# Attention in another order: all sequence items, then all memory items

## The reference

```python
u = rms_norm(x, g_mix) @ w_in            # split into lru, gate, q, k, v, qm
y_lru = rg_lru(conv(u_lru)) * gelu(u_gate)
q, k = rms_norm(u_q), rms_norm(u_k)      # 6 query heads, 2 key heads, 64 wide
y_swa = sliding_window_sink_attention(q, k, v, sinks)   # window 128, blocks of 128
mkv = rms_norm(mem, g_mem) @ w_mem_kv    # 256 memory tokens
y_mem = memory_cross_attention(qm, km, vm)              # 4 heads, softmax over 256
y = concat(rms_norm(y_lru), rms_norm(y_swa), rms_norm(y_mem))
h = x + y @ w_out
h = h + moe(rms_norm(h))                 # 32 experts, top 4 of a router
```

## Time and profile before

| | |
|---|---|
| time before, median of 3 runs | 2288.44 us (2286.68 to 2290.86) |
| time of the profiled execution | 2293.3 us |
| its span, first to last instruction | 2291.6 us |
| mean granted TensorE clock | 0.978 |
| busy: TensorE, its weight loads | 2175.5 us (95%), 1609.1 us (70%) |
| busy: VectorE, ScalarE, GpSimd | 1422.4 us (62%), 1094.1 us (48%), 227.6 us (10%) |
| attention and its token sums | 262.7 to 384.8 us |
| chain that ended last | TensorE 73%, VectorE 8%, issue 7%, ScalarE 6%, DMA 4% |

### The profile page before, as it was taken

The page is one execution under the profiler, slowest core; times in us unless marked ns, Lnnn a source line. Parts: engine busy times, 40 slices in busy tenths (PEclk is TensorE's granted clock), DMA queues, the critical chain, the costliest instruction groups (busy, mean ns, idle before and its releaser), DMA issues.

```text
span 2291.6 us, 31520 instructions
## 1 busy us (share of the span) xinstructions
PE 2175.5 (95%) x9748; PEld 1609.1 (70%) x9749; DVE 1422.4 (62%) x2152; ACT 1094.1 (48%) x1602; POOL 227.6 (10%) x208
## 2 busy tenths in 40 slices
PE   6999988996999999999999999999999999999997
PEld 4443776443578877776787878787778877887885
DVE  3342573334775677768767575768786657667665
ACT  3241452112464465556555454546565445445444
POOL 2000200002210011011101010110100110101001
PEclk9999997996999999999999999999999999999998
DMA  7000402002795589869958586858997658658556
GB/s 254 1 0 19 157 1 74 28 28 88 275 362 195 187 277 332 289 205 348 343 177 322 182 297 198 290 183 326 353 335 265 204 174 297 196 177 315 181 182 220
DMA packets 203190, 477.62 MB, mean 208 GB/s; under 512 B 14744, under 2 KB 20952, under 8 KB 203089
## 3 DMA queue, kind: packets, MB, share of 16 engines
q1 hardware_dynamic: 185662, 437.95, 52.7%
q0 software_dynamic: 17424, 39.17, 7.5%
q10 hardware_dynamic: 66, 0.02, 0.0%
HBM read 468.73 MB, written 32.11 MB: 219 GB/s over the span
## 4 chain that ended last, share of the span: by engine, by line
PE 73%; DVE 8%; issue 7%; ACT 6%; DMA 4%; DVEq 1%; POOLq 1%; ACTq 0%; POOL 0%; SPq 0%
PE ps L1107 15%; PE ps L1109 15%; PE ps L1108 15%; PE ps L878 7%; PE ps L1032 5%; DMA out<-y,idx_cur 4%; DVE w_lo L1576 3%; PE ps L1168 3%; ACT w_hi L752 2%; PE ps L1143 2%; PE ps L1161 1%; PE ps L1101 1%; PE ps L983 1%; PE ps L951 1%; DVE hm L1636 1%
## 5 line engine op out<-in xcount | busy, mean ns | idle before, releaser
L1576 DVE TENSOR_TENSOR w_lo<-ring,w_hi 128x1024 fp32r<-128x1024 f32 x692 | 815.5, 1219 | 182.1 <-ACT w_hi L752 178.7
L752 ACT ACTIVATE w_hi<-ring 128x1024 fp32r<-128x1024 f32 x692 | 696.4, 1055 | 295.9 <-PE ps L1109 277.1
L1107 PE MATMUL ps<-w_hi,xT_hi 128*128 128x512 f32 x1288 | 512.6, 398 | 20.5 <-ACT y L778 15.2
L1109 PE MATMUL ps<-w_hi,xT_lo 128*128 128x512 f32 x1288 | 503.3, 391 | 0.0
L1108 PE MATMUL ps<-w_lo,xT_hi 128*128 128x512 f32 x1288 | 503.1, 391 | 0.0
L1107 PEld LDWEIGHTS ps<-w_hi,xT_hi 128*128 128x128 f32 x1288 | 242.4, 188 | 81.8 <-issue 32.5
L1107 PE MATMUL ps<-w_hi,actT_hi 128*128 128x512 f32 x720 | 289.4, 402 | 0.0
L1109 PE MATMUL ps<-w_hi,actT_lo 128*128 128x512 f32 x720 | 281.9, 392 | 0.0
L1108 PE MATMUL ps<-w_lo,actT_hi 128*128 128x512 f32 x720 | 281.2, 390 | 0.0
L1108 PEld LDWEIGHTS ps<-w_lo,xT_hi 128*128 128x128 f32 x1288 | 242.2, 188 | 55.2 <-issue 4.5
L1109 PEld LDWEIGHTS ps<-w_hi,xT_lo 128*128 128x128 f32 x1288 | 242.2, 188 | 51.7
(11 more groups left out here) (262 smaller groups left out, 1997.4 us busy)
## 6 DMA issues: line engine op xcount, KB each, us to landing
ring<-in_w SPq DMA_DIRECT2D x390, 1024.0 KB, 7.2
xh<-in_x SPq DMA_DIRECT2D x4, 2048.0 KB, 15.7
work<-in_w_out SPq DMA_DIRECT2D x1, 4096.0 KB, 12.9
token_rows<-uT POOLq DMA_DIRECT2D x8, 512.0 KB, 2.9
out<-xh SPq DMA_DIRECT2D x8, 512.0 KB, 2.7
work<-in_w_in SPq DMA_DIRECT2D x2, 1536.0 KB, 18.4
uT<-in_w_mem_kv SPq DMA_DIRECT2D x1, 2048.0 KB, 13.7
ring<-in_w_in SPq DMA_DIRECT2D x1, 1536.0 KB, 18.7
```

The source lines that it names most:

```text
L752: act_e.activation(w_hi[h % SPLIT][:, :, :], part(h), ACT.Copy).then_inc(hi_ready, counted(h, whole))
L1107: pe.matmul(acc, hi, whi, start=first, stop=False)
L1109: return pe.matmul(acc, lo, whi, start=False, stop=last)
L1576: return dve.tensor_tensor(lo, x, hi.bitcast(F32), ALU.subtract)
```

## The change

The list of items is written in another order: all eight sequence blocks, then all eight memory blocks. Nothing else in the stage is edited; every engine's program, its waits and their counts are derived from the list. The sums of squares of the items' outputs stand in 16 columns in the order of the items, so the view that separates the two kinds changes with it.

```diff
-        items = [(kind, b) for b in range(NT) for kind in ("swa", "mem")]
+        items = [("swa", b) for b in range(NT)] + [("mem", b) for b in range(NT)]
...
             link(dve.tensor_scalar(grp[:, 0:8], ps[:, 0, 0:NT], 1.0 / DL, EPS, ALU.mult, ALU.add))
-            sso = st[:, 96:112].rearrange("p (b two) -> p two b", two=2)
+            sso = st[:, 96:112].rearrange("p (two b) -> p two b", two=2)
             link(dve.tensor_scalar(grp[:, 8:16], sso[:, 0, :], 1.0 / DL, EPS, ALU.mult, ALU.add))
             dve.tensor_scalar(grp[:, 16:24], sso[:, 1, :], 1.0 / (NM * DH), EPS, ALU.mult, ALU.add).then_inc(grp_ms, 1)
```

## The result

The changed kernel takes 2300.38 us (median of 5 runs, 2297.72 to 2302.93), the kernel before 2288.44 us (median of 5): the ratio is 1.0051, with a 95% interval of 1.0038 to 1.0063, or +8.7 to +14.4 us. It is slower, as forecast, by 11.9 us by the medians where +16.9 was forecast; 2300.4 lies within the range.

What follows compares the result with a forecast made beforehand. The prediction took the attention stage to be bound by a chain of waits, with ScalarE's copy behind the next item's exponentials. Terms 6.9 + 12.0 - 2.0 = +16.9 us on 2288.4 gave 2305 us, range 2291 to 2314.

Steps and rivals of the forecast that it cites:

- What bounds the stage: Attention stage: no engine is full; a chain of waits sets the time, ScalarE's copy standing behind the next item's exponentials.
- Term one: Attention stage at full clock: 9.74 us per sequence item plus 4.86 per memory item in place of 13.63 a pair; +6.9 us.
- Term two: Sequence items: TensorE's clock falls to half in four of six stretches, 3.0 us each; +12.0 us, between 0 and 18.
- I take 3.0: Cost in us of one clock fall: a sequence item's last four transposes and the next scores all at half rate.
- the whole 4.5 us: Sequence loop: stretch from the end of the values to the next scores, where TensorE does nothing but transposes, six times.
- The tail: End of the attention stage: both last items are now memory items, shorter and perhaps longer at full clock; -2.0 us.
- The clock holds: Rival: no clock fall in the sequence loop, term two is 0, tail gains perhaps 4; +3 us, 2291 us; chance 0.12.
- The low clock sticks: Rival: scores do not bring the clock back, six sequence loops run slow; +29 us, 2317 us; chance 0.09.
- TensorE's work bounds the new order: Rival: ScalarE's copy does not wait behind exponentials; sequence item 6.8 us, memory item 4.7; gains 14.9 us, 2274; chance 0.05.

Runs made afterwards that it cites:

- the extra matmuls: Changed kernel plus 18 unneeded 128x128 matmuls before the last four transposes of sequence item 1, ten before those of items 2 to 6: 2292.64 us, ratio 1.0018 to before.
- one item ahead on ScalarE: Changed kernel with ScalarE's exponentials issued one item ahead instead of two, so item j's copies precede item j+1's exponentials: 2270.86 us, ratio 0.9923 to before.

## Why the prediction was right, and where it was off

**What bounds the stage**: right. A copy behind the exponentials of the next item closes the loop; taking it from behind them took 29.5 us away, 21.7 of them between the first late turn and the last. The same edit helps the order of before, which the prediction had described as bound by that very copy.

**Term one, +6.9 us**: right. The body without any fall is 100.1 us (99.7 worked out) against 92.9: +7.2.

**Term two, the clock, +12.0 us**: the mechanism was right and its size was off. Three, four and three falls came where four were taken, and each cost less: the body's mean over three profiles is 106.4, which is 6.3 us above 100.1, 1.9 us a fall in place of 3.0. The step that failed is "I take 3.0": it let the whole late turn and all scores run at half clock. That happened in one fall of ten, whose loop took 12.74 us in place of 9.75. Elsewhere the clock came back within the scores, so only part of them ran slowly. Six falls left it low for 3.4 us and cost 1.3 to 1.7 us each, four left it low for 6.8 us and cost 2.2 to 3.0. Before has falls of its own, two in four profiles, 0.6 us on average. So the term measured is +5.7.

The Trainium skill ("TensorE: Matmul & The Clock Gate", "Why this matters for your kernels") says that idle gaps between bursts of matmuls return the clock to half rate. The prediction read the whole 4.5 us as one, but TensorE does transposes in it and is idle for 4.4 us ahead of item 1's late turn and for 2.7 us ahead of the others. Item 1's stretch fell in three profiles of three, the others in seven cases of fifteen, so the trace agrees in part.

**The tail, -2.0 us**: mean 22.7 us in place of 26.0, so -3.3. Of the split, up to 5 us for the clock was about right (27.8 against 21.8 us, and 24.2 against 19.5), while 1 us for the kind of item was too little (3.6 and 2.3). One reading of rows was wrong: the prediction has the clock fall between 357.0 and 360.5, but the earlier trace rows have it at 1.00 there. It fell at 361.6, 1.1 us into the last sequence values, so that stretch is no case of a fall ahead of the values. And the tail of the profiled execution of before, 27.8 us, was among its longest, so a comparison with that one profile alone overstates the gain.

The terms as measured: 7.2 + 5.7 - 3.3 = +9.6 us, against +11.9 by the medians, inside the interval of 8.7 to 14.4. The seven profiled executions that they come from differ by 9.5 us on average themselves (2299.9 us in three against 2290.4 in four), so the terms account for them; the remaining 2.3 us is which executions were profiled. Against these terms the forecast is 7.3 us too high: 6.3 in term two and 1.3 in the tail, less 0.3 in term one. That it misses the medians by only 5.0 is luck of the executions profiled.

**The rivals.** "The clock holds" did not come true in any profile of the changed kernel; with the extra matmuls it did, and that kernel is 4.0 us above before, near the +3 given for it. "The low clock sticks": it came back within the scores in nine falls of ten, and 0.1 us behind them in the tenth. "TensorE's work bounds the new order" was refuted by the 9.75 us loops; one item ahead on ScalarE is the way to it, with 7.39 us against the 6.8 that it named.

## What to carry to other kernels

In a hand-ordered pipeline, look at what stands on each queue between an instruction and what it waits for, by kind of item: alternating a long and a short item can hide a badly placed copy, and grouping them shows it. The better repair is often the queue's own order and not the order of the items: here moving the exponentials one item later was worth 17 us in the order of before and 29 us in the changed one, while the order itself was worth 12. Where a new wait leaves TensorE idle for several us, price the clock too, by falls that a trace shows: here a fall cost 1.3 to 3.0 us, and 1.9 on average, where a burst of 3.0 us was at risk.

## What was not expected of the hardware

In the kernel before, the nearly idle 2.9 us ahead of the first memory item's values left the clock at 1.00 in two profiles. In the two others it fell about 2 us behind the start of these values, at 275.7 and 273.5 us, with TensorE at work. The third profile of before, by windows:

```profile
272.00:275.40 3.40, 1.85 (x17) 1.85 (x18) 1.89 (x3) 3.40 (x14) 0.00 (x0) 1.00 0.96 384
275.60:278.90 3.30, 3.30 (x17) 2.91 (x16) 1.86 (x7) 1.29 (x4) 0.00 (x0) 0.52 0.00 0
```

The falls of the changed kernel came at the same items in three profiles, and at others where the same loop ran in another program; what decides is open. And real matmuls that compute nothing of use, 4.2 us of them in the longest idle stretch and 2.4 us in the others, kept the clock at 1.00 over 111 us without delaying the late turn.
